# Half-chunk loads of the weights and other orders around the norms, the attention and the long convolution, in a two-block fp32 kernel

## The reference

```python
def first_block(x, ...):
    h = rms_norm(x, g_mix_pre[l])
    q, k, v, p_in, gm_u, gm_v, gate_in = jnp.split(h @ w_in[l], IN_SPLITS, axis=-1)
    ...  # stick-breaking attention, pooling, chunked spatial gating
    merged = gates[..0] * (o_sb @ w_br_sb[l]) + gates[..1] * (o_pool @ w_br_pool[l]) + gates[..2] * (o_gm @ w_br_gm[l])
    x = x + rms_norm(merged @ w_out[l], g_mix_post[l])
    h = rms_norm(x, g_ff_pre[l])
    ff = jnp.square(jax.nn.relu(h @ w_ff_in[l])) @ w_ff_out[l]        # 1024 -> 4096 -> 1024
    return x + rms_norm(ff, g_ff_post[l])

def second_block(x, c, ctx, c_ctx, w_mod, ...):
    mod_x, mod_c = silu(c) @ w_mod + b_mod, silu(c_ctx) @ w_mod + b_mod   # six shifts, scales, gates
    hx, hc = modulate(rmsnorm(x), ...), modulate(rmsnorm(ctx), ...)        # ctx: 256 tokens
    ...  # 4 heads of differential attention (two softmax maps each) over 256 + 512 keys, with RoPE
    ...  # hyena: 12 groups of 128 columns, short conv, two gated long convolutions by Fourier transform
    x = x + g_a * (concat([attn, hyena]) @ w_out)
    x = x + g_f * conv_ffn(modulate(rmsnorm(x), ...))                      # 1024 -> 2 x 2816 -> 1024
    return rmsnorm(x, final_norm)
```

## Time and profile before

| | us |
|---|---|
| median of 3 runs (lowest, highest) | 1669.24 (1667.66, 1671.48) |
| the profiled execution, by the same clock as the runs | 1674.56 |
| its span, on which the positions below are counted | 1672.5 |
| PE busy in it | 1551.4 (93%) |
| DVE, ACT, POOL busy | 877.4, 618.5, 268.6 |
| mean granted clock of PE | 0.967 |

### The profile page before, as it was taken

One profiled execution on the slowest core, in us unless ns is written; L12 is line 12 of the kernel. 1 busy time (PEld: TensorE's weight loads), 2 busy tenths in 40 slices (PEclk: granted clock), 3 DMA queues, 4 the chain that ended last, 5 costly groups with the idle time before them and its releaser, 6 DMA issues.

```text
span 1672.5 us, 17467 instructions
## 1 busy us (share of the span) xinstructions
PE 1551.4 (93%) x6918; PEld 1230.3 (74%) x6918; DVE 877.4 (52%) x1387; ACT 618.5 (37%) x964; POOL 268.6 (16%) x269
## 2 busy tenths in 40 slices
PE   6999999889989898999997998888879899999998
PEld 5776668678778677887876786566658688888886
DVE  6446555444476454664445326672774645345544
ACT  5445653222443211234234324453333433223332
POOL 0352111011002100021001310001642111021101
PEclk9999999899999899999998999997989999999999
DMA  6341003434353442444324220021531322222221
GB/s 231 115 160 51 26 25 140 188 127 149 126 176 130 148 150 101 176 141 161 126 95 147 101 76 25 26 101 51 175 131 71 114 101 84 99 94 101 101 101 51
DMA packets 34410, 187.96 MB, mean 112 GB/s; under 512 B 3896, under 2 KB 4408, under 8 KB 16474
## 3 DMA queue, kind: packets, MB, share of 16 engines
q1 hardware_dynamic: 27514, 165.88, 28.3%
q0 software_dynamic: 3456, 12.58, 2.5%
q10 hardware_dynamic: 3360, 8.39, 1.4%
HBM read 174.25 MB, written 12.58 MB: 112 GB/s over the span
## 4 chain that ended last, share of the span: by engine, by line
PE 67%; DVE 14%; ACT 7%; issue 5%; DMA 4%; POOL 3%; SPq 0%; ACTq 0%; DVEq 0%; POOLq 0%
PE PS L428 66%; DMA raw<-in_ws 3%; DVE wl L1638 3%; ACT wh L1065 2%; DVE accm L1617 2%; POOL TMP L2296 1%; ACT em L1432 1%; DVE smallring L2053 1%; DVE TMP L2150 1%; DVE TMP L2074 1%; PE PS L439 1%; DVE em L2067 1%; DVE TMP L2154 0%; DMA kd<-TMP 0%; DMA X<-in_x 0%
## 5 line engine op out<-in xcount | busy, mean ns | idle before, releaser
L1638 DVE TENSOR_TENSOR wl<-raw,wh 128x1024 fp32r<-128x1024 f32 x223 | 288.2, 1297 | 348.5 <-ACT wh L1065 348.5
L428 PE MATMUL PS<-HTh,wh 128*128 128x512 f32 x1056 | 422.3, 400 | 10.7 <-ACT TMP L1363 6.5
L428 PE MATMUL PS<-HTl,wh 128*128 128x512 f32 x1056 | 414.8, 393 | 0.0
L428 PE MATMUL PS<-HTh,wl 128*128 128x512 f32 x1056 | 414.5, 393 | 0.0
L1065 ACT ACTIVATE wh<-raw 128x1024 fp32r<-128x1024 f32 x228 | 239.1, 1055 | 418.1 <-PE PS L428 243.9
L428 PEld LDWEIGHTS PS<-HTh,wh 128*128 128x128 f32 x1056 | 200.8, 190 | 60.9 <-issue 7.7
L428 PEld LDWEIGHTS PS<-HTh,wl 128*128 128x128 f32 x1056 | 200.3, 190 | 43.5
L428 PEld LDWEIGHTS PS<-HTl,wh 128*128 128x128 f32 x1056 | 200.8, 190 | 38.7 <-issue 0.5
L428 PE MATMUL PS<-wh,FFh 128*128 128x512 f32 x432 | 172.3, 399 | 4.8 <-DVE Y L1919 2.8
L428 PE MATMUL PS<-wl,FFh 128*128 128x512 f32 x432 | 170.8, 395 | 0.0
L428 PE MATMUL PS<-wh,FFl 128*128 128x512 f32 x432 | 170.5, 395 | 0.0
(11 more groups left out here) (323 smaller groups left out, 2192.0 us busy)
## 6 DMA issues: line engine op xcount, KB each, us to landing
raw<-in_ws SPq DMA_DIRECT2D x134, 1024.0 KB, 4.9
taps<-TMP SPq DMA_DIRECT2D x16, 256.0 KB, 2.5
tab<-in_spec POOLq DMA_DIRECT2D x8, 512.0 KB, 5.1
raw<-taps SPq DMA_DIRECT2D x4, 1024.0 KB, 4.8
kd<-TMP ACTq DMA_DIRECT2D x16, 256.0 KB, 3.4
kf<-kd SPq DMA_DIRECT2D x8, 512.0 KB, 3.3
wh<-in_wd POOLq DMA_DIRECT2D x8, 512.0 KB, 4.0
wl<-in_wd POOLq DMA_DIRECT2D x8, 512.0 KB, 4.7
```

The costliest lines, as they stand in the source:

```text
L428: return nc.tensor.matmul(out, l, r, start=start, stop=stop, skip_group_check=True)
L1638: tt(WL[k][:, :n], RAW[RAW_NO[j] % 2][:, o:o + n], f32(WH[k][:, :n]), ALU.subtract).then_inc(sem("lo_dve"), 1)
```

## The change

1. **Loads of half a chunk.** `RAW` becomes four places of 1024 columns. A load brings one unit (512 KB), or one half of a mod; it waits for the low part of the unit (or the adds of the half mod) that was four loads before it in its place.
2. **Spectra.** `put_spectrum` moves from ACT's program to POOL's, into its queue; RoPE takes the slots 2 to 4 in place of 4 to 6, and `spread` gets a tile of its own (`SPR`). DVE's `spectrum(0, 0)` moves from ahead of the low parts `HTl` of n2 to behind the fourth of them, `spectrum(1, 0)` into n3 behind its second tile. A part 0 takes the banks that pieces 1 to 4 of the out-product had.
3. **Around the norms.** In the tails of w_out, w_ff_out and w_out_2 the weights of the next units are made one at a time behind rows 2 and 3 of the tail, where before several were made ahead of row 3. The 8 copies of the first half of w_ff_out go from DVE to ACT ("fo_c"). The transposes of the context stand between the k-steps of the second `w_ff_out` (`context`), in two banks.
4. **Low parts.** The second "taps" units (four) are added to those that POOL makes, one unit (156) is taken from it.
5. **Attention.** `diff_max` takes one maximum for each map, with a scale behind each (64 instructions where there were 32), and ACT's first exponential waits for its own map alone. The quarters of hyena groups go two at a step from the first step on. The product with V goes to whichever of banks 6 and 7 the current group doesn't use, no longer to bank 5.
6. **Convolution.** Hyena groups 8 and 9 take banks 6 and 7. `sub_scale` of heads 0 and 2 takes a bank of `ACC`, that of head 0 stands behind `forward(0, 0)`. Group 10 stands ahead of the last two `backward`. w_out_2's first four banks are those of `RING4`, the transposes of n5 those of `ACC`, and n4 takes the banks in the order of w_out_2's.

The diff, cut to its core:

```diff
+RAWS = 4
-RAW_NO = {j: i for i, j in enumerate(j for j, (kind, _) in enumerate(PLAN) if kind != "pre")}
+RAW_AT = {}
+for _u in range(NU):
+    for _i, _m in enumerate(MODS):
+        if _m[2] == _u:
+            for _h in range(2):
+                RAW_AT["mod", _i, _h] = len(RAW_AT)
+    if _u not in PRE:
+        RAW_AT["unit", _u, 0] = len(RAW_AT)
+LOADS = list(RAW_AT)
...
-        RAW = [at("raw", 48 + 8 * i, [P, CHUNK]) for i in range(2)]
+        RAW = [at("raw", 48 + 4 * i, [P, UNIT]) for i in range(RAWS)]
...
-                r = loaded[0] % 2
-                if loaded[0] >= 2:
-                    before = RAW_CHUNKS[loaded[0] - 2]
-                    if PLAN[before][0] == "mod":
-                        e.wait_ge("mod_acc", MOD_PARTS[i][1])
+                if n >= RAWS:
+                    was, y, g = LOADS[n - RAWS]
+                    if was == "mod":
+                        parts, steps = MOD_PARTS[y]
+                        e.wait_ge("mod_acc", steps - 4 * len(parts) * (1 - g))
                     else:
-                        e.wait_ge(*lows(LAST_UNIT[before]))
+                        e.wait_ge(*lows(y))
...
-                    engine.dma_start(RAW[r][:, :w], a["ws"][j, :, :w]).then_inc(sem(f"d_raw{r}"), 16)
+                    engine.dma_start(RAW[r][:, :w], a["ws"][j, :, o:o + w]).then_inc(sem(f"d_raw{r}"), 16)
...
-                    for n in range(2):
-                        weights(unit("w_ff_out", 15 * P, n * S) + SLOTS - 1)
-                        for i in range(4):
-                            e.wait_ge("p_fo", 4 * n + i + 1)
-                            nc.vector.tensor_copy(half(Y, i, n), PS[:, BANK[("fo", 0), 4 * n + i], :]).then_inc(sem("fo_y"), 1)
+                    weights(unit("w_ff_out", 15 * P, S) + SLOTS - 1)
...
-                    e.wait_ge(f"d_kd{4 + r}", 32)
+                    e.wait_ge(f"d_kd{2 + r}", 32)
...
+            weights(unit((0, 1, 3), 0, 0))
+            put_spectrum(0, 0)
...
+                if q == 1:
+                    put_spectrum(0, 1)
...
+            for part in range(2):
+                put_spectrum(1, part)
...
-                nc.vector.reduce_max(r[:, 0:2], s, axis=mybir.AxisListType.X).then_inc(sem("df_mx"), 1)
-                e.wait_ge("df_mx", 2 * n + 1)
-                ts(r[:, 0:2], r[:, 0:2], -0.125, None, ALU.mult).then_inc(sem("df_mx"), 1)
+                for m in range(2):
+                    s = PS[:, 2 * m:2 * m + 2, :].rearrange("p a n -> p (a n)")[:, 0:768]
+                    nc.vector.reduce_max(r[:, m:m + 1], s, axis=mybir.AxisListType.X).then_inc(sem("df_mx"), 1)
+                    e.wait_ge("df_mx", 4 * n + 2 * m + 1)
+                    ts(r[:, m:m + 1], r[:, m:m + 1], -0.125, None, ALU.mult).then_inc(sem("df_mx"), 1)
...
-                b = bank(("dv", h), "dv_ev", h + 1, (5,))
+                b = bank(("dv", h), "dv_ev", h + 1, (13 - BANK["hy", (ahead - 1) // 4],))
...
-                bank(("hy", j), "hc_v", 6 * j + 6, RING4)
+                bank(("hy", j), "hc_v", 6 * j + 6, RING2 if j < 10 else RING4)
...
-                b = bank(("sn", h), "sn_v", h + 1, RING4)
+                b = bank(("sn", h), "sn_v", h + 1, RING4 if h % 2 else ACC)
...
-            banks0 = [bank(("o2", i), "o2_v", i + 1) for i in range(4)]
+            banks0 = [bank(("o2", i), "o2_v", i + 1, RING4) for i in range(4)]
```

More of the change, by code:

```diff
@@ L727, in spectrum @@
                 e.wait_ge(f"d_tab{part}", 32 * (o + 1))
-                among = first_part(o) if part else None
+                if part:
+                    among = first_part(o)
+                else:
+                    among = tuple(BANK["out" if o == 0 else ("fo", 1), i] for i in range(1, 5))
                 for f in range(2):
@@ L780, in tensor_program, with context @@
                     i.then_inc(sem("p_ff"), 1)
-                if hf:
-                    for q in range(4):
-                        b = bank(("nc", q), "nc_za", 2 * q + 2)
+                def context(j):
+                    if j % 3 == 2 and j < 12:
+                        q = j // 3
+                        out = [BANK[("fo", 1), i] for i in range(4)]
+                        b = bank(("nc", q), "nc_za", 2 * q + 2, tuple(x for x in turns[0] if x not in out)[:2])
                         for k in (2 * q, 2 * q + 1):
@@ L1025, in turn_n4 @@
                 return m
+            order = tuple(BANK["o2", i] for i in range(8))
             for k in range(7):
-                bank(("n4", k), *shifted_out("n4")(k))
+                bank(("n4", k), *shifted_out("n4")(k), order)
                 turn_n4(k, (0, 1, 2))
@@ L1982, in vector_program @@
             weights(unit((1, 1, 3), 0, 0) + SLOTS - 1)
+            for i in range(added[0], len(MODS)):
+                close_mod(i)
+            e.wait_ge("mod_add", 8 * 2 + 16)
+            stt(AFF, MOD[:, 32:40], 1.0, pp("norm_ffn_2", 0, 8), ALU.add, ALU.mult).then_inc(sem("ax"), 1)
             def spread(s):
@@ L2481, in load @@
                 loaded[0] += 1
             def weights(upto):
-                while unit_at[0] <= min(upto, NU - 1):
-                    u = unit_at[0]
-                    while mod_at[0] < len(MODS) and MODS[mod_at[0]][2] == u:
-                        load()
-                        mod_at[0] += 1
-                    if u not in PRE and LAST_UNIT[UNITS[u][0]] == u:
-                        load()
-                    unit_at[0] += 1
+                while loaded[0] < len(LOADS):
+                    kind, x, _ = LOADS[loaded[0] - RAWS]
+                    if (x if kind == "unit" else MODS[x][2]) > upto:
+                        return
+                    load()
@@ L2497, in sync_program @@
             engine.dma_start(PPT[:, :], a["pp"]).then_inc(sem("d_c"), 16)
-            load()
-            load()
+            for _ in range(RAWS):
+                load()
             engine.dma_start(TMP[0:33, 0, :], a["zt"]).then_inc(sem("d_f"), 16)
```

272 lines of the change are left out of this document (141 added, 131 removed).

## The result

The changed kernel takes 1589.31 us (median of 4 runs, 1589.01 to 1590.69), beside 1668.76 us (1667.66 to 1671.48) of the kernel before. The ratio is 0.9523, with a 95% interval from 0.9507 to 0.9540: 79.5 us faster. 1593.3 us had been predicted. The profiled execution took 1589.17 us, of which 1587.4 are its span, 85.4 us less than the profiled execution of before.

A forecast was written before the change was run, and what follows sets the result against it. TensorE, busy 1551.4 of 1672.5 us, was taken as the bound. Gains of 17.6 (gates), 21.3 (first FFN), 14.5 (norms), 4.5 (attention) and 18 (convolution) sum to 75.9: 1669.2 - 75.9 = 1593.3 us, 8 in 10 range 1575 to 1634.

The forecast's parts named there:

- Gates: 250 to 360 us: two stalls from late weight loads, gaps plus half-speed work, both taken as gone with half-chunk loads; 17.6 us.
- First FFN: 560 to 675 us: four stalls, gaps plus half-speed work, taken at 9.6, 2.5, 5.8 and 3.4; sum 21.3 us.
- the stall at the heavy mods: First FFN, 595:608: mods of 16 adds fill DVE and `flush` still comes behind them; 2.5 taken of 7.1 us.
- Norms: w_out's tail 2, the stretch ahead of w_ff_out 2.5 and w_ff_out's tail 10; all norms 14.5 us.
- w_ff_out's tail: 870:912: `rope`'s wait for a kd store becomes one for short part 0 stores; 10 us taken from 8 to 16.
- Attention: 1011:1130 us: PE idles 19.2 us; bounds 0 and 10, 4.5 us taken, near the sum of three bank-5 gaps.
- the three gaps: Attention: three gaps of 1.5 us, transposes waiting for DVE's L2047, reader of bank 5; the change takes them out.
- Convolution: 1130 to 1252 us: three stalls at 1141:1160, 1162:1171 and 1241:1252, sum 21; 18 us taken.
- (1): Whole kernel: stalls shortened, not removed, and half-speed pieces remain; half of 75.9 us realised, 1631 us; chance 0.25.
- (2): Gates and first FFN: half loads served one at a time make the kernel slower, 1709 us at 4.2 each; chance 0.04.
- the prediction's own formula: Gates and first FFN: 122 loads at p us beside 396 us of PE, 76 us gains given up; break-even p 3.9.
- (3): POOL's added low parts and stores disturb DVE and the reverse; up to 9 us, some at PE, 1602 us; chance 0.09.

## Why the prediction was right, point by point

**Gates.** Right in cause and size: 17.7 for 17.6. The half loads alone give it, and with whole chunks the load behind bc and X explains less than half of the first gap. What the prediction gave no weight in its sum is that several loads must be in flight: one at a time, the gates take 139.0 us of the 141.0.

**First FFN.** 24.6 for 21.3. In these two traces the term that was mis-sized is the stall at the heavy mods, put at 2.5 of 7.1 us: it gave 5.8, since the gap fell from 3.68 to 1.27 and the whole piece at half speed behind it went. The others came out as in the sum: 9.6 in the first stall, 5.8 at the copies, 3.5 at the last. The trial with the copies back on DVE gave 5.9 for them. Two things make the 24.6 less firm than it looks. Against the other four traces of this FFN as it was before, the gain is 17.3 to 21.5. And in three later kernels with the same FFN as the changed one (stores in ACT's queue and both orders of the convolution) the gap of 1.27 is followed by 3.4 us at 0.5, and the FFN takes 173.1 us. So the 21.3 is as good as the 24.6, and whether the term of 2.5 was too small stays open.

**Norms.** 16.1 for 14.5. w_out's tail gave 0.7 for 2. The second w_ff_in gave 4.6 for 2.5: 3.3 are the two gaps, and the other 1.3, with the context's transposes now between k-steps, were not looked into. w_ff_out's tail gave 10.8 for 10. Its mechanism was right, that `rope` would wait for an earlier store; most of it is the slots, 1.4 us the queue.

**Attention.** 8.6 for 4.5, and here the step failed in its cause. I had taken the three gaps of 1.5 us as the gain and the maxima as next to nothing. The maxima gave 3.7 us of gaps in the attention's 16 steps, and 1.6 by the clock; the bank gave 0.6 of gaps, and 1.7 by the clock that can't be put down to it. I had even written that the next hyena group waits for the same reader, and not drawn the sum from it. 2.1 of the 8.6 lie ahead of the 16 steps. In three of the kernels that share this attention it takes 205.0 us with 6.8 at half speed, not 202.3, and then the gain is 5.9, so how near the forecast came is partly chance.

**Convolution.** 18.4 for 18. The bank of groups 8 and 9, put at 10.5 (4.43 and 6.1), gives 7.6 us in the trace by itself, as half of its piece at half speed stays. The bank of w_out_2 gives 7.3 there only with the rest of the change, which was not foreseen; and group 10's new place leaves a gap of 5.02 us ahead of head 3's scale, for which the prediction had held back 3 us.

**The rivals.** (1) Gaps shortened rather than removed: that is what is left in the two tails and at 1126 to 1138, while in gates and FFN they went. (2) Slower by serial half loads: they are not serial, and even when made so the kernel is not slower than before. Their median of 3.6 us was close to the 3.3 of the earlier trace rows. By the prediction's own formula 3.6 gives 1669 + 439 - 472 = 1636 us, and 1632 was measured; that it is so near is luck, since the stretches with loads took more than 122 times 3.6 (139.0 us from unit 28 to 50 and 337.5 from 62 to 116, 476.5 in all beside 439), while the gains of the other stages, which the formula gives up, stayed. The price that the formula gave for breaking even, 3.9 us, was never reached. The Trainium skill's rule in "DMA: Bandwidth & Descriptors", section Bandwidth, to use 1 MiB or more, holds here for the price (3.8 us for half of what took 4.9) but not for the choice: the kernel moves the same bytes in 95% of the time. (3) POOL beside DVE: DVE's two-input lines of `spectral` reach 2.8 and 2.9 us at most, as before. One new case appeared, DVE's L1872 beside POOL's HCl. The line's instructions in the changed kernel (ns min/median/max):

```profile
L1872 DVE TENSOR_SCALAR Y<-X,smallring x8: 752/753/2209, 428.8 to 831.2; 128x1024 f32<-128x1024 f32 x8
```

and one of them in DVE's timeline, with the one in POOL's timeline that runs beside it:

```profile
825.24 2.21 DVE L1872 TENSOR_SCALAR Y<-X,smallring 128x1024 f32<-128x1024 f32 x1
...
824.49 2.40 POOL L2412 TENSOR_TENSOR HCl<-zc,HCh 128x1024 fp32r<-128x1024 f32 x1 [20.27 <-PE PS L444]
```

It took 2.21 us once where its median is 0.753, 1.5 us in w_ff_out's tail, far from the 9 of the rival. In the version with the tail's edits, where HCl stands elsewhere, all 8 took 0.752 to 0.754.

**The sum** was 9.5 us too small against the profiled execution (75.9 for 85.4), and 4.0 us off in the median, since the profiled execution of before lay 5.8 us above its median. So the hit on 1593 is partly luck: terms that were too small in the attention and, by these traces, the FFN stand against gains that the long execution of before made look larger than they are in the median.

## What to carry to other kernels

Where a double buffer is freed by the last of several consumers, halve its pieces at the same bytes: each load may then start a consumer earlier, and it also passes other transfers in the queue. Keep several of them in flight, for one at a time gave back nearly all of it here. More bytes were not tried. Before moving a reader or a bank, ask who takes the freed bank next and who is next in the turn; two of these edits gave next to nothing alone because the wait only changed its owner. Cost a stall as the gap and the piece at half speed behind it, but expect the second part to come and go between executions, and take the gain of a stretch from more than one trace.
